# Turning the attention maxima with one matmul a block and moving the row by small DMAs

## The reference

```python
def block_attention(q, k, v, n_kv):
    B, S, H, dq = q.shape
    scale = dq ** -0.5
    ...
    def one_block(qblk):
        s = jnp.einsum('bqkgd,blkd->bkgql', qblk, k).astype(jnp.float32) * scale
        p = jax.nn.softmax(s, axis=-1).astype(v.dtype)
        return jnp.einsum('bkgql,blkd->bqkgd', p, v)
    ...

mo = block_attention(mq, kv[0], kv[1], MLA_HEADS)
go = block_attention(gq, kv[2], kv[3], GQA_KV_HEADS)
```

## Time and profile before

| | us |
|---|---|
| median of three runs | 3118.92 (3114.74 to 3126.46) |
| profiled execution | 3113.74 |
| its span, first to last instruction | 3111.9 |
| TensorE busy | 2955.8 (95%) |
| VectorE busy | 2268.6 (73%) |
| GpSimd busy | 1403.8 (45%) |
| ScalarE busy | 1335.0 (43%) |

### The profile page before, as it was taken

How to read it: one execution, slowest core, us unless ns; L and a number is a source line. 1 busy time by engine, 2 the same in 40 slices (tenths; PEclk the granted TensorE clock), 3 DMA queues, 4 the chain that set the end, 5 groups by cost and what they waited for, 6 DMA issues and landing times. The chain is left out here.

```text
span 3111.9 us, 43216 instructions
## 1 busy us (share of the span) xinstructions
PE 2955.8 (95%) x15921; PEld 2224.9 (71%) x15921; DVE 2268.6 (73%) x3178; ACT 1335.0 (43%) x1903; POOL 1403.8 (45%) x835
## 2 busy tenths in 40 slices
PE   5999967999999999999999979999999999999997
PEld 3889854566656666665657858888788888888786
DVE  4445455778787877878766888777777758787778
ACT  3223223344444444444452446555555544433441
POOL 1333313577785967766661334333333235323420
PEclk7999988999999999999999989999999999999999
DMA  6232389325343243433026777446544497887783
GB/s 257 59 93 74 95 257 271 102 59 130 93 109 86 49 92 84 90 93 71 14 95 216 272 271 269 149 150 250 209 149 149 161 332 282 306 312 291 285 305 139
DMA packets 246124, 526.54 MB, mean 169 GB/s; under 512 B 29680, under 2 KB 104944, under 8 KB 234736
## 3 DMA queue, kind: packets, MB, share of 16 engines
q1 hardware_dynamic: 239408, 498.23, 49.4%
q10 hardware_dynamic: 6528, 25.82, 2.1%
HBM read 363.19 MB, written 160.76 MB: 168 GB/s over the span
## 5 line engine op out<-in xcount | busy, mean ns | idle before, releaser
L1261 DVE TENSOR_REDUCE h_mpart<-a_mx 128x1 f32<-128x512 f32 x920 | 537.5, 632 | 188.1 <-PE a_mx L1358 174.6
L1240 ACT ACTIVATE a_pf<-o_y 128x1024 f32<-128x1024 f32 x432 | 442.0, 1026 | 496.0 <-PE o_y L1397 489.3
L1194 POOL TENSOR_TENSOR a_acc_p<-a_acc_p,a_pf 128x1024 f32<-128x1024 f32 x240 | 577.9, 2408 | 163.0 <-ACT a_pf L1240 135.2
L2406 PE MATMUL f_bank<-slots,f_wx 128*128 128x512 f32 x2304 | 533.6, 392 | 13.0 <-DMA slots<-s_uc 7.5
L2414 PE MATMUL f_bank<-slots 128*128 128x512 f32 x2352 | 537.3, 389 | 3.3 <-DVE slots L2185 3.3
L2406 PEld LDWEIGHTS f_bank<-slots,f_wx 128*128 128x128 f32 x2304 | 435.9, 189 | 105.7 <-DMA slots<-s_uc 8.9
L2414 PEld LDWEIGHTS f_bank<-slots 128*128 128x128 f32 x2352 | 441.0, 188 | 96.4 <-DVE slots L2185 4.8
L2352 POOL TENSOR_TENSOR f_work<-raw_rows 128x512 f32<-128x512 f32 x160 | 220.9, 1382 | 378.9 <-DVE f_wx L2178 367.1
L2361 POOL TENSOR_TENSOR f_y<-f_y,raw_rows 128x1024 f32<-128x1024 f32 x72 | 203.3, 2823 | 335.1 <-DMA raw_rows<-in_w 335.1
L2199 DVE TENSOR_TENSOR f_work<-f_work,f_bank 128x512 f32<-128x512 f32 x256 | 174.4, 681 | 134.7 <-ACT f_work L2077 123.9
L553 PE MATMUL p_main<-win_hi,u_hi 128*128 128x512 f32 (+2 forms) x528 | 197.9, 375 | 15.2 <-PEq L75 14.5
(11 more groups left out here) (274 smaller groups left out, 5130.9 us busy)
## 6 DMA issues: line engine op xcount, KB each, us to landing
raw_rows<-s_hx SPq DMA_DIRECT2D x112, 512.0 KB, 4.2
f_y<-in_w SPq DMA_DIRECT2D x104, 512.0 KB, 5.3
raw_rows<-in_w SPq DMA_DIRECT2D x72, 512.0 KB, 6.0
raw_rows<-in_w SPq DMA_DIRECT2D x32, 1024.0 KB, 4.9
s_hx<-stream SPq DMA_DIRECT2D x128, 256.0 KB, 2.7
s_hx<-f_work SPq DMA_DIRECT2D x96, 256.0 KB, 2.2
raw_rows<-in_w_ada SPq DMA_DIRECT2D x8, 2048.0 KB, 8.5
low<-s_mix SPq DMA_DIRECT2D x32, 512.0 KB, 5.5
```

The costliest lines, as they stand in the source:

```text
L1194: nc.gpsimd.tensor_tensor(acc[:, :], left[:, :], pf[(b * KT + kt) % NPF][:, :], ALU.add).then_inc(added_p, 1)
L1240: nc.scalar.activation(pf[n % NPF][:, :], sc[n % 2][:, :], ACT.Exp, scale=SCALES[0 if is_mla(b) else 1]).then_inc(exped, 1)
L1261: nc.vector.reduce_max(mpart[b % 2][:, s + 4 * half, k:k + 1], bank(("pair", c), half)[:, 0:CHUNKS[k][1]], AX.X).then_inc(mx_read, 1)
L2406: mm = nc.tensor.matmul(by_pair(bank[:, m % 8, :]), w[:, k], x[s][:, :, k * P:(k + 1) * P], start=(k == 0 and j == 0), stop=(k == 3 and j ...
```

## The change

The maxima of a block are turned by a single matmul (`turn_row`), whose weights are a new zeroed window `mturn` with the eight columns side by side. Its result is 8 lines of 128. ScalarE copies these into a small tile `turned`, and SyncE moves each line by a DMA of 512 bytes into its place in `max_row` or `mq` (`move_row`). The turn stands behind the values of step 11, right after the last pair (in block 0 after the scores of step 14). `max_row` becomes two tiles in turn; the second is filled with zeros by GpSimd at the start. The first block's row is laid by the eight matmuls as it was. The step rule `spots_of` is changed so that block 22 too has its last pairs in its second batch.

```diff
-            c0, c1 = (upto[b] + due * n // NBATCH for n in (batch, batch + 1))
+            c0, c1 = (upto[b] + min(due, max(due, NI) * n // NBATCH) for n in (batch, batch + 1))
...
+        ROW_AT = lambda b: 2 * BATCH - 1 if b else ADA_TURN
+        rows_set = lambda b: 16 * QT * b
...
+            def move_row(b):
+                sp.wait_ge(row_copied, b + 1)
+                sp.wait_ge(padded, PADS)
+                if b >= 2:
+                    sp.wait_ge(scored, KT * (b - 1))
+                for half, strip in enumerate(STRIPS):
+                    line = slice(strip.start + ROPE, strip.start + ROPE + 1) if is_mla(b) else slice(strip.start, strip.start + 1)
+                    to = mq[b % NBLK][line, R_HM, :] if is_mla(b) else max_row[b % NBLK][line, :]
+                    for t in range(QT // 2):
+                        r = half * (QT // 2) + t
+                        sp.dma_start(raw(to[:, t * P:(t + 1) * P]), raw(turned[r:r + 1, :])).then_inc(row_set, 16)
...
+                if b + 1 < NSB:
+                    move_row(b + 1)
                 if b == NSB - 2:
                     sp.wait_ge(ada_done, 2 * len(MOD_BLOCKS))
...
-                for tile, fill in [(rk_lm[rest, :], 1.0)] + [(mq[blk][rest, R_HM, :], 0.0) for blk in range(NBLK)]:
+                for tile, fill in [(max_row[1][strip, :], 0.0), (rk_lm[rest, :], 1.0)] + [(mq[blk][rest, R_HM, :], 0.0) for blk in range(NBLK)]:
...
             def row(b):
-
                 act.wait_ge(row_done, b + 1)
-                at = bank(("row", b))
-                if not is_mla(b):
-                    nc.scalar.activation(max_row[:, :], at, ACT.Copy).then_inc(row_set, 1)
-                    return
-                act.wait_ge(padded, PADS)
-                for strip in STRIPS:
-                    line = slice(strip.start + ROPE, strip.start + ROPE + 1)
-                    nc.scalar.activation(mq[b % NBLK][line, R_HM, :], at[line, :], ACT.Copy).then_inc(row_set, 1)
+                need(act, row_set, rows_set(b - 1))
+                nc.scalar.activation(turned[:, :], bank(("row", b))[0:QT, 0:P], ACT.Copy).then_inc(row_copied, 1)
...
+                    if kt == ROW_AT(b) + 1 and b + 1 < NSB:
+                        row(b + 1)
                     act.wait_ge(scored, n + 1)
...
-                nc.vector.reduce_max(by_tile(mcol[:, 32:32 + BLK])[:, :, 0], mpart[b % 2][:, :, :], AX.X).then_inc(col_set, 1)
+                to = mturn[:, 0:QT] if b else by_tile(mcol[:, 32:32 + BLK])[:, :, 0]
+                nc.vector.reduce_max(to, mpart[b % 2][:, :, :], AX.X).then_inc(col_set, 1)
...
+            def turn_row(b):
+                pe.wait_ge(col_set, b + 1)
+                bank_free(pe, ("row", b))
+                nc.tensor.matmul(bank(("row", b))[:, 0:P], mturn, g.minus_ident_r[:, :], start=True, stop=True).then_inc(row_done, 1)
...
                     if kt == 0 and m == len(ops) - 1:
-                        pe.wait_ge(row_set, rows_before(b + 1))
+                        if b:
+                            pe.wait_ge(row_set, rows_set(b))
+                        else:
+                            pe.wait_ge(row_copied, 1)
+                        pe.wait_ge(padded, PADS)
...
-                    if kt == KT - 1 and b + 1 < NSB:
-                        lay_row(b + 1)
...
                         for s in range(kt - BATCH + 1, kt + 1):
                             values(b, s)
+                        if b and kt == ROW_AT(b) and b + 1 < NSB:
+                            turn_row(b + 1)
```

More of the change, by code:

```diff
@@ L993, in stage_attend @@
         KPE_HI, KPE_LO = 4, 2
-        rows_before = lambda b: sum(2 if is_mla(n) else 1 for n in range(b))
+        ROW_AT = lambda b: 2 * BATCH - 1 if b else ADA_TURN
+        rows_set = lambda b: 16 * QT * b
         freed, bank_of = [], {}
@@ L1001, in banks @@
             freed.extend(ends)
-        banks(("row", 0), (row_set, rows_before(1)))
+        banks(("row", 0), (row_copied, 1))
         for b in range(NSB):
@@ L1010, in stage_attend @@
                     banks("gate", *(2 * [(w_gated, 2 * KD)]))
-                if kt == KT - 1 and b + 1 < NSB:
-                    banks(("row", b + 1), (row_set, rows_before(b + 2)))
                 if kt == BATCH - 1 and b:
                     banks(("den", b - 1), (nrm_set, b))
+                if kt == ROW_AT(b) and b + 1 < NSB:
+                    banks(("row", b + 1), (row_copied, b + 2))
                 if b in MOD_BLOCKS and kt == ADA_BATCH:
@@ L1231, in weight_high @@
                 nc.scalar.activation(g.wo_hi[k], g.rows[k % len(g.rows)], ACT.Copy).then_inc(g.w_hi_set, 1)
-            row(0)
+            first_row()
             for b in range(NSB):
@@ L1244, in _ @@
                         weight_high(W_HIGHS[kt])
-                if b + 1 < NSB:
-                    row(b + 1)
                 copy_o(b)
@@ L1361, in pair, with lay_first_row @@
                             mm.then_inc(mx_done, 1)
-            def lay_row(b):
-                pe.wait_ge(col_set, b + 1)
-                bank_free(pe, ("row", b))
-                at, first = bank(("row", b)), 0 if is_mla(b) else 32
+            def lay_first_row():
+                pe.wait_ge(col_set, 1)
+                at = bank(("row", 0))
                 for r in range(2):
                     for s in range(4):
-                        col = first + (4 * r + s) * P - DH * r
+                        col = 32 + (4 * r + s) * P - DH * r
                         mm = nc.tensor.matmul(at[:, s * P:(s + 1) * P], mcol[:, col:col + P], g.minus_ident_r[:, :],
@@ L1448, in _ @@
                         modulation_columns(i)
+                    if b == 0 and kt == ROW_AT(b):
+                        turn_row(b + 1)
                     if b == W_BLOCK and kt == 0:
```

23 lines of the change are left out of this document (14 added, 9 removed).

## The result

| | us |
|---|---|
| after, median of six runs | 3102.05 (3095.01 to 3108.44) |
| before, median of the six runs beside it | 3118.47 (3114.74 to 3126.93) |
| ratio after / before | 0.9943, 95% interval 0.9928 to 0.9958 |
| profiled execution after | 3108.44, span 3106.6 |

The account below looks back on a forecast made before the run. TensorE, busy 1090.4 of 1112.0 us in the attention stretch, was taken as the bound, VectorE next. 24.3 removed - 4.3 for turns - 4.2 given back = 15.8 us, so 3118.92 becomes 3103.1 us; range 3095 to 3113.

Parts of the forecast that it names:

- The eight matmuls, 1.01 us each time: After a block's last step: eight shifted matmuls at L1370 removed 23 times, 1.01 us each, 23.2 us in all.
- The turn, 0.25 us, paid 17 times: One added 128x128 matmul between values and scores, 23 times; 0.25 us each, paid in 17, 4.3 us.
- The upper one, 0.52: Upper bound for the added matmul: 0.13 plus 0.39 us of idle time like that ahead of L1370.
- the row of L1438: Lower bound for the added matmul: 8 records from 757.79, scores at 758.77, 0.12 us each with the change of form.
- The wait of block 22: TensorE's 1.07 us wait for block 23's maxima column goes with the changed step rule; the pairs only move.
- Given back at block changes: VectorE's denominator additions get less time, so TensorE waits longer at five block changes: 4.2 us, ends 2.0 and 8.
- Block 0: swallowed: GpSimd's fills hold TensorE from 528.25 to about 530.2; the later 6.78 us wait for modulation weights swallows the 2 us.
- The row in time: Eight 512-byte DMAs a block on SyncE cost nothing; in block 3 the row has 0.3 to 2.8 us to spare.
- A: TensorE's slack all taken by VectorE and the forms: 0.52 a turn, 8 us at block changes, 3111; chance 0.16.
- B: The turn hides nearly everywhere (0.05 a block or less) and VectorE catches up: 21.3 us less, 3097.6; chance 0.12.
- C: The row comes late, the eight DMAs going one after the other: 104 us lost, 3207; chance 0.06.
- D: The edit does nothing for the end, since the eight matmuls run under a wait: 3118; chance 0.02.

Follow-up runs that it names:

- the doubled row: The kernel before, with the eight shifted matmuls issued twice for each of the 23 later rows; 3139.76 us, ratio 1.0071.
- the run in which the clock held there: The changed kernel with two DMAs a block in place of eight, each moving four lines; 3103.2 us.

## Why the prediction was right

**The eight matmuls, 1.01 us each time: right.** A block saves 0.73 to 0.83 in most blocks, which is 1.01 less the turn, and 1.02 to 1.13 where the turn is free; the doubled row gives 0.112 a matmul and 0.11 once. Blocks 2, 6, 10 and 18 save 0.88 to 0.93, and that is the larger half of the 1.1 by which -18.3 is more than -17.2. In these, and in 19, the values started 1.46 to 1.48 us behind the last matmul of a pair before, and 1.35 to 1.40 in the others; after it is 0.32 everywhere. So the eight took 0.1 more there; why is open.

**The turn, 0.25 us, paid 17 times: right.** From values to pair are 5.56 us where they were 5.30, so 0.26, in all 22 blocks with the turn in that place. The Trainium skill, "TensorEngine Tiling (Array Packing)", Key Properties, has the array drain at a change of mode; it has no price for that. The trace agrees that a further change costs something: 0.26 less the 0.112 of a repeated matmul leaves about 0.15, by estimate. Neither of my bounds was well read, and that 0.25 lay so near is in part luck. The upper one, 0.52, used idle time of 8.6 us over 22 cases that the earlier trace rows has for the weight loads at L1370; its matmuls come just 0.24 us later than a pair's length would have them (716.70 to 717.17 in the earlier trace rows). And the row of L1438, which I followed, is of matmuls with 2 columns, and I read only the step behind it: ahead of it the last scores start at 757.28 and it starts at 757.79, 0.28 more than a pair takes. The five blocks in which I had it free are those that save over 1 us. ScalarE's copy took 0.27 us and held nobody.

**The wait of block 22: half right.** It went, as the step said, but "the pairs themselves only move" was wrong. In a third batch without pairs TensorE waits for ScalarE's exponentials, and about 0.45 us of the 1.07 come back.

**Given back at block changes, 4.2 us forecast, 7.3 measured: the mis-sized term.** The places were right: 3 to 4 (+2.23), 7 to 8 (+2.61), 11 to 12 (+1.06), 15 to 16 (+1.13), 10 to 11 (+0.31), and nowhere else. The mechanism was right too: the wait in block 4 grew by just 1.01 us, and the doubled row removed it. What I put at nothing is that a wait of TensorE may cost more than its length. At 727 and at 911 the granted clock falls behind waits of 1.66 and 1.96 us, and TensorE runs at its lower level for 3.4 us. At 3 to 4 that is 2.23 less the 1.01 of longer wait, 1.2 us, and the run in which the clock held there shows the same difference. At 7 to 8 the wait is 1.40 longer, 0.4 more than was taken out, which leaves 1.2 us for the clock. Clock and longer wait are together 2.8 of the 3.1 by which the term was short. The rest is 11 to 12 and 15 to 16, at 1.1 and not 0.9. How much of this comes in another trace is not sure: with two DMAs the clock held in one of the two places. With 7.3 the forecast's sum would have been 12.7.

**Block 0: swallowed, as forecast, but more than one thing.** The score matmuls wait for the fills 1.8 us, and the clock, at half until 528 us before, stays there until 539:

```profile
532.71 1.10 POOL L1159 MEMSET a_mq<- 32x512 f32 x2
533.95 0.80 PE L1419 MATMUL o_y<-h_max_row,ones_f 64*128 64x512 f32 x2 [1.81 <-POOL a_mq L1159]
...
566.50 1.56 PE L850 MATMUL a_mx<-raw_rows,cond_pad 128*32 128x512 f32 x5 [2.50 <-DMA raw_rows<-in_w_ada]
```

The first values come 16.22 us behind the first laid row instead of 12.37, and the wait for the weights takes 2.50 instead of 6.78. So 4.3 of the cover of 6.8 us were used, by a cost I had at 2.

**The row in time: right.** In block 3 SyncE starts at 713.8, and its issues follow each other at 0.63 (0.49 forecast), so the last starts at 718.25. It lands 3.1 us later, between the bounds of 2.4 and 4.9, and the row is in place at 721.4, where it is needed at 724.26: 2.9 us to spare (0.3 to 2.8 forecast), and 2.7 in block 7. The first of the eight took 6.0 us. The Trainium skill, "DMA: Bandwidth & Descriptors", Anatomy of one DMA, gives a fixed cost of about 2.0 us for one DMA, measured on GpSimd's path. These go by SyncE, and over all blocks the trace has 1.7 at the least, 2.1 in the median and 7.4 at most. Eight of them cost their issues and one landing, not eight times that.

**Rivals.** A was near with its give-back (8 us, 7.3 measured), but not with waits at nearly every block change, and with 0.52 a turn it failed; B's free turn failed at 0.26; C and D are out by the experiments.

**The sum.** -13.5 in the stage against -15.8 forecast, -17.8 (-22.5 to -13.1) by the ratio. The forecast lies in the interval, but part of that nearness is luck. Within the stage 1.1 us more from the eight matmuls hide a third of what the block changes cost too much. The stage accounts for 13.5, and whether the other 4 us of the ratio are more than the spread outside the stage stays open.

## What to carry to other kernels

Work taken from the fullest engine is worth its pitch where nothing waits behind it, and little or nothing where a wait does; the list of waits tells the places, here five of twenty-three, and an engine that is just in time counts as one of them. A longer wait may also lower TensorE's clock behind it (here 3.4 us at half, for 1.2 us of time), so that removing work there can lose time; leave the work in at those places, or shorten what is waited for (here a store behind a 2 MB load). When small DMAs replace such work, count their issues one by one and their landing once.

## What was not expected of the hardware

- TensorE's granted clock fell from full to 0.50 for 3.4 us behind waits in a stretch where it was otherwise busy: behind 1.66 and 1.96 us in the changed kernel, behind 1.65 in the one with two DMAs, behind two waits of 0.65 and 0.80 and two of 0.94 and 0.72 in the one with sixteen, and behind 1.07 us and sixteen small matmuls in the one with the doubled row. It held behind 1.69 in the kernel with two DMAs, behind 1.17 to 1.50 in the kernel before, and behind all waits of 0.98 and less that stood alone. So the length of the wait alone doesn't decide it, and no run here tells what does.
- Three additions of 128x1024 on VectorE took 4.07 us with GpSimd's convolution cut down, 5.8 with it, and 6.1 to 7.1 where the late cast had moved GpSimd's own addition beside them. One that stood beside an operation of GpSimd ended 1.07 to 1.09 us behind it, in all five cases given above.
- SyncE's DMAs of 512 bytes from one place of the on-chip memory to another follow each other at 0.63 us. The last of eight landed 1.7 us behind its issue in 15 of 23 blocks and 2.9 to 5.4 in the other eight.
